# Recurrent gates on two row tiles of 64 partitions, with both gates' weights of a head side by side

## The reference

```python
def rg_lru(x, wa, ba, wx, bx, lam):            # x: (1, 1024, 1024); wa, wx: (16, 64, 64)
    xh = x.reshape(bsz, s, LRU_HEADS, LRU_HEAD_DIM)      # 16 heads of 64 channels
    r = jax.nn.sigmoid(jnp.einsum('bshi,hij->bshj', xh, wa).reshape(bsz, s, c) + ba)
    i = jax.nn.sigmoid(jnp.einsum('bshi,hij->bshj', xh, wx).reshape(bsz, s, c) + bx)
    log_a = -RG_C * r.astype(jnp.float32) * jax.nn.softplus(-lam.astype(jnp.float32))
    a = jnp.exp(log_a)
    mult = jnp.sqrt(-jnp.expm1(2.0 * log_a))
    b = mult * (i * x).astype(jnp.float32)
    ...                                        # h[t] = a[t] * h[t-1] + b[t], over the 1024 tokens
```

## Time and profile before

| | |
|---|---|
| median of 3 runs | 1730.13 us (1728.16 to 1732.98) |
| span of the profiled execution | 1726.5 us |
| TensorE busy | 1681.0 us, 97% |
| VectorE busy | 1225.3 us, 71% |
| ScalarE busy | 792.4 us, 46% |
| GpSimd busy | 516.6 us, 30% |
| mean HBM traffic over the span | 102 GB/s |

### The profile page before, as it was taken

One profiled execution on the slowest core, in us unless ns is written; L12 is line 12 of the kernel. 1 busy time (PEld: TensorE's weight loads), 2 busy tenths in 40 slices (PEclk: granted clock), 3 DMA queues, 4 the chain that ended last, 5 costly groups with the idle time before them and its releaser, 6 DMA issues.

```text
span 1726.5 us, 20915 instructions
## 1 busy us (share of the span) xinstructions
PE 1681.0 (97%) x7556; PEld 1383.3 (80%) x7556; DVE 1225.3 (71%) x1442; ACT 792.4 (46%) x1038; POOL 516.6 (30%) x284
## 2 busy tenths in 40 slices
PE   7999999999999999999999999998999999999998
PEld 6888878888877888888888888886878877777776
DVE  6577772259999888888888789885636365666554
ACT  5466541235764434343434455553322146676531
POOL 4221222200015555554552000003432242345320
PEclk8999999999999999999999999999999999999999
DMA  8111112152422232222223876651321320110251
GB/s 259 49 36 49 40 45 74 37 201 80 152 81 76 83 97 73 84 84 87 73 86 125 317 237 199 219 159 43 122 74 61 85 86 25 37 49 25 102 215 73
DMA packets 161095, 176.96 MB, mean 102 GB/s; under 512 B 13566, under 2 KB 114692, under 8 KB 161028
## 3 DMA queue, kind: packets, MB, share of 16 engines
q1 hardware_dynamic: 158724, 167.67, 30.3%
q10 hardware_dynamic: 2304, 8.39, 1.3%
HBM read 140.38 MB, written 35.65 MB: 102 GB/s over the span
## 4 chain that ended last, share of the span: by engine, by line
PE 82%; DVE 10%; ACT 4%; issue 1%; POOL 1%; DMA 1%; POOLq 0%; DVEq 0%; ACTq 0%; SPq 0%
PE ps L921 28%; PE ps L2398 24%; PE ps L2352 18%; PE ps L2618 4%; PE ps L2603 3%; PE ps L2648 2%; PE ps L2588 1%; DVE lat L2109 1%; PE ps L2576 1%; DVE pt_lo L2203 1%; DVE prob L2185 1%; POOL z_lo L1015 1%; PE ps L2279 1%; DVE square_dve L1636 0%; ACT pt_hi L1548 0%
## 5 line engine op out<-in xcount | busy, mean ns | idle before, releaser
L945 POOL TENSOR_TENSOR w_lo<-w_raw,w_hi 128x1024 fp32r<-128x1024 f32 x52 | 135.8, 2614 | 623.0 <-ACT w_hi L1044 623.0
L2398 PE MATMUL ps<-hop_hi_P,wop_hi_P 128*128 128x512 f32 x672 | 262.5, 391 | 4.7 <-DVE u L1853 3.3
L2398 PE MATMUL ps<-hop_hi_P,wop_lo_P 128*128 128x512 f32 x672 | 261.5, 389 | 0.0
L2398 PE MATMUL ps<-hop_lo_P,wop_hi_P 128*128 128x512 f32 x672 | 261.5, 389 | 0.0
L921 PE MATMUL ps<-h_hi,w_hi 128*128 128x512 f32 x752 | 235.1, 394 | 11.3 <-DVE h_lo L1621 7.8
L951 POOL TENSOR_TENSOR wop_lo_P<-pair_sum,wop_hi_P 128x512 fp32r<-128x512 f32 x90 | 135.9, 1510 | 354.5 <-ACT wop_hi_P L1055 354.5
L921 PE MATMUL ps<-h_lo,w_hi 128*128 128x512 f32 x752 | 232.9, 391 | 0.0
L921 PE MATMUL ps<-h_hi,w_lo 128*128 128x512 f32 x752 | 232.7, 391 | 0.0
L921 PEld LDWEIGHTS ps<-h_hi,w_hi 128*128 128x128 f32 x752 | 141.4, 189 | 43.3 <-issue 14.0
L921 PEld LDWEIGHTS ps<-h_lo,w_hi 128*128 128x128 f32 x752 | 142.1, 189 | 29.8
L921 PEld LDWEIGHTS ps<-h_hi,w_lo 128*128 128x128 f32 x752 | 142.0, 189 | 29.7
(11 more groups left out here) (350 smaller groups left out, 3337.9 us busy)
## 6 DMA issues: line engine op xcount, KB each, us to landing
pair_raw<-in_w_up SPq DMA_DIRECT2D x48, 512.0 KB, 4.6
w_raw<-in_w_in SPq DMA_DIRECT2D x46, 512.0 KB, 3.9
dn_raw<-gu_park SPq DMA_DIRECT2D x84, 256.0 KB, 3.9
dn_raw<-in_w_down SPq DMA_DIRECT2D x60, 256.0 KB, 3.1
gu_park<-up_cv SPq DMA_DIRECT2D x24, 512.0 KB, 2.6
out_raw<-in_w_out SPq DMA_DIRECT2D x30, 256.0 KB, 3.0
x_tok<-in_x SPq DMA_DIRECT2D x4, 1024.0 KB, 8.2
x_park<-xs SPq DMA_DIRECT2D x1, 4096.0 KB, 14.3
```

The costliest lines, as they stand in the source:

```text
L945: nc.gpsimd.tensor_tensor(lo[:, :], raw[:, :], hi[:, :].bitcast(f32), ALU.subtract).then_inc(w_lo_done, 1)
L2398: mm = nc.tensor.matmul(dst, w[q][:, k, :], x[q][:, k, :], start=a, stop=b, skip_group_check=True)
```

## The change

The gates of a tile are no longer a matmul with a block-diagonal matrix. Each of the two heads of a tile is a matmul of its own on 64 rows, with 128 columns of weights: 64 of `wa` and 64 of `wx`, side by side. The even head lies on partitions 0 to 63 and writes `ps[2]`, the odd one on partitions 64 to 127 and writes `ps[3]`; their matmuls are issued alternately. The number of matmuls stays 12 in a tile.

The columns of the odd head are in the other order (`which ^ e`), so that gate r of both heads comes out on the head's own partitions. Gate i then comes out on the other half, and ScalarE moves it: the two Tanh of 128 partitions become four of 64, and `bx` is kept with its halves exchanged. The block of zeros goes, and with it the memset, the wait for it and half of the columns of the gate weights that are cast and subtracted.

```diff
-        bd_raw = at("bd_raw", G0 + 8 * TILE, [2, LRU_TILES, P])
-        bd_hi = at("bd_hi", G0 + 10 * TILE, [2, P], f32r)
-        bd_lo = at("bd_lo", G0 + 11 * TILE, [2, P], f32r)
+        head_raw = at("head_raw", G0 + 8 * TILE, [LRU_TILES, P])
+        head_hi = at("head_hi", G0 + 10 * TILE, [P], f32r)
+        head_lo = at("head_lo", G0 + 11 * TILE, [P], f32r)
...
-            sp.wait_ge(const_done, BD_ZEROED)
             for which, wg in enumerate((lru_wa, lru_wx)):
                 heads = wg.rearrange("o (c e) i j -> (o e) i c j", e=2)
                 for e in range(2):
-                    sp.dma_start(bd_raw[64 * e:64 * e + 64, which, :, 64 * e:64 * e + 64],
-                                 heads[e]).then_inc(bd_in, 16)
+                    first = 64 * (which ^ e)
+                    sp.dma_start(head_raw[64 * e:64 * e + 64, :, first:first + 64], heads[e]).then_inc(bd_in, 16)
...
-            nc.gpsimd.memset(bd_raw[:, :, :, :], 0.0).then_inc(const_done, 1)
...
             def gate_weights(c, one):
-                nc.scalar.copy(bd_hi[:, :, :], bd_raw[:, :, one, :].rearrange("p w o n -> p w (o n)")
-                               ).then_inc(bd_hi_done, 1)
+                nc.scalar.copy(head_hi[:, :].unsqueeze(1), head_raw[:, one, :]).then_inc(bd_hi_done, 1)
 
             def gate_curves(c, one):
 
-                act.wait_ge(ri_done, 2 * c + 1)
-                nc.scalar.activation(scr[1][:, :], ps[2][:, :], ACT.Tanh, scale=0.5,
-                                     bias=half_ba[:, one]).then_inc(rt_done, 1)
+                even, odd = slice(0, 64), slice(64, P)
                 act.wait_ge(ri_done, 2 * c + 2)
-                nc.scalar.activation(scr[2][:, :], ps[3][:, :], ACT.Tanh, scale=0.5,
-                                     bias=half_bx[:, one]).then_inc(it_done, 1)
-
-                act.wait_ge(rt_done, c + 1)
+                for head, bank in ((even, ps[2]), (odd, ps[3])):
+                    nc.scalar.activation(scr[1][head, :], bank[head, :], ACT.Tanh, scale=0.5,
+                                         bias=half_ba[head, one]).then_inc(rt_done, 1)
+                for head, other, bank in ((even, odd, ps[2]), (odd, even, ps[3])):
+                    nc.scalar.activation(scr[2][head, :], bank[other, :], ACT.Tanh, scale=0.5,
+                                         bias=crossed_bx[other, one]).then_inc(it_done, 1)
+
+                act.wait_ge(rt_done, 2 * c + 2)
...
-            step(V.tensor_scalar(half_bx[:, :], vec[:, V_BX:V_BX + 8], 0.5, None, ALU.mult))
+            for head, other in ((slice(0, 64), slice(64, P)), (slice(64, P), slice(0, 64))):
+                step(V.tensor_scalar(crossed_bx[other, :], vec[head, V_BX:V_BX + 8], 0.5, None, ALU.mult))
...
             def second_parts(c, one):
                 dve.wait_ge(bd_hi_done, c + 1)
-                step(V.tensor_tensor(bd_lo[:, :, :], bd_raw[:, :, one, :].rearrange("p w o n -> p w (o n)"),
-                                     bd_hi[:, :, :].bitcast(f32), ALU.subtract))
+                step(V.tensor_tensor(head_lo[:, :].unsqueeze(1), head_raw[:, one, :], head_hi[:, :].bitcast(f32).unsqueeze(1),
+                                     ALU.subtract))
...
             def gates():
-                matmul3(pe, ps[2], bd_hi[:, 0, :], bd_lo[:, 0, :], xc_hi, xc_lo, True, True).then_inc(ri_done, 1)
-                matmul3(pe, ps[3], bd_hi[:, 1, :], bd_lo[:, 1, :], xc_hi, xc_lo, True, True).then_inc(ri_done, 1)
+                for w, x, first, last in ((head_hi, xc_hi, True, False), (head_hi, xc_lo, False, False),
+                                          (head_lo, xc_hi, False, True)):
+                    for t in (T1, T2):
+                        for head, bank in ((slice(0, 64), ps[2]), (slice(64, P), ps[3])):
+                            mm = nc.tensor.matmul(bank[:, t], w[head, :], x[head, t], start=first, stop=last)
+                            if last and t is T2:
+                                mm.then_inc(ri_done, 1)
```

More of the change, by code:

```diff
@@ L316, in program @@
         half_ba = const("half_ba", 8)
-        half_bx = const("half_bx", 8)
+        crossed_bx = const("crossed_bx", 8)
         half_ps = const("half_ps", 4)
@@ L360, in program @@
         const_done, vec_t, vec_done, setup_done = sem("const_done"), sem("vec_t"), sem("vec_done"), sem("setup_done")
-        IDENT, BD_ZEROED, SMALL_CONST, ALL_CONST = 1, 2, 7, 23
+        IDENT, SMALL_CONST, ALL_CONST = 1, 6, 22
         SIGN, POS_F, LAM_ABS, PARAMS = 4, 5, 6, 7
@@ L1685, in recur @@
                 step(V.tensor_scalar(scr[3][:, :], scr[1][:, :], -2.0, -1.0, ALU.mult, ALU.add))
-                dve.wait_ge(it_done, c + 1)
+                dve.wait_ge(it_done, 2 * c + 2)
                 step(V.scalar_tensor_tensor(out=scr[2][:, :], in0=scr[2][:, :], scalar=1.0, in1=xc,
@@ L2337, in _ @@
                 if n < 4:
-                    pe.wait_ge((conv_done, gelu_done, rt_done, it_done)[n], LRU_TILES)
+                    pe.wait_ge((conv_done, gelu_done, rt_done, it_done)[n], (1, 1, 2, 2)[n] * LRU_TILES)
                 else:
```

## The result

The changed kernel took 1746.18 us (median of 4 runs, 1744.07 to 1746.96), beside 1730.56 us for the kernel before (4 runs). The ratio is 1.0084, 95% interval 1.0067 to 1.0102: slower by 0.84%; the two medians lie 15.6 us apart. The forecast was 1737.4 us, slower by 0.42%, with a range from 1733 to 1748. The sign, the place and the mechanism were right; the forecast loss of 7.3 us is less than half of those 15.6.

A forecast was written before the change was run, and what follows sets the result against it. TensorE paces the kernel except at 248.76 us, where block 2 awaits a chain over ScalarE and VectorE. Loop +2.0, last two tiles +3.9 and slow clock +1.4 give +7.3 us: 1737.4 us, range 1733 to 1748.

The forecast's parts named there:

- Matmuls: Gates on TensorE: each pair of 64-row matmuls runs side by side in 0.227 us, 1.36 us per tile for 2.72.
- The serial rival: The two row tiles run one after the other, 26.18 us per loop iteration: +16.2 us, 1746.3 us; chance 0.18.
- The likeliest case: Whole kernel slower by 0.42%: 1737.4 us, with its own range 1735 to 1741 us; chance 0.50.
- Curves: Gate activations on ScalarE: two of 128 partitions become four of 64 at full time each, 2.00 us more per tile.
- The ring: Loop over recurrent tiles: ScalarE's curves, VectorE's recurrence to `xc_lo`, then gate matmuls set the pace, 24.82 us per iteration.
- The tail: From tile 6's first curve to block 2 of the short convolution: 37.5 us becomes 41.4, two tiles' extra curve time less 0.1.
- The gap and its clock: Ahead of block 2 TensorE idles 5.5 us instead of 1.5; the low clock behind it adds 1.4 us.
- Behind 248.8 us nothing takes it back: After block 2 starts TensorE has no gap, so the later start carries through to the total in full.

The follow-up runs named there:

- the first four experiments: Changed kernel with whole curves, 1724.14 us; kernel before with split curves, 1747.87; changed kernel with gate i whole, 1734.51; changed kernel with 18 unread matmuls, 1739.72.
- full_curves: The changed kernel with two Tanh of 128 partitions in place of its four of 64: 1724.14 us, ratio 0.9975 to the kernel before.

## Why the prediction was half right

*Matmuls: right.* 0.227 us per pair was taken, on no row of before; 1.59 us for the twelve was measured, where 1.36 to start and 1.52 to finish were expected. The serial rival gave 1746.3 us, the measured total to 0.1 us, and this is chance: its mechanism is excluded by the rows at 61.65 us. It was also this rival that set the upper end of the range, 1748 us. The likeliest case had 1735 to 1741 us as its own range, so that the measured time lies within the stated range is luck.

*Curves: right in kind, too small in size. This is the step that failed.* "ScalarE does 2.00 us more per tile" came from the start-to-start time of whole activations. Whole ones overlap: each lasts 1.12 us and the next starts after 1.00. Halves don't; each follows the end of the last, 1.135 us. The extra is 4.54 - 2.00 = 2.54 us. The row was there, in ScalarE's timeline of the kernel before:

```profile
1432.22 2.12 ACT L1501 CAST qr<-scr 64x1024 fp32r<-64x1024 f32 x2 [0.72 <-DVE scr L2129]
...
1447.34 1.93 ACT L1509 CAST qh_hi<-ps 128x1024 fp32r<-128x1024 f32 x2
```

A pair of 64-partition casts, as in the earlier trace rows, takes 2.12 us, a pair of 128 partitions in the same stretch 1.93. I had read a duration and priced it with a spacing.

*The ring: right.* The gate ring paces the loop, as forecast, and TensorE waits for `xc_lo`. With 0.54 more for the curves my 24.82 us become 25.36, and 25.22 was measured. The curve of tile 6 came at 215.74, not 213.3.

*The tail: right.* 41.4 us from there to block 2 were forecast, 42.55 measured, and 2 x 0.54 us of curves is the difference. Block 2 was 9.5 us later, not 5.9. Of the 3.6 us between, that one price alone would make 8 x 0.54 = 4.3; the first curve came 0.58 us earlier (64.04 us), which takes most of the surplus back.

*The gap and its clock: right at its place, missed elsewhere.* The gap was forecast at 5.5 us and was 4.24, since `xc_lo` of tile 7 came 0.5 us later and the matmuls behind its 2.2 us gap ran slowly. It cost 2.1 us for the 1.4 assumed. But the forecast looked for a low clock only there. The clock also fell behind the 2.21 us gap ahead of the gates of tile 7, near 500 us, and behind the 2.13 us gap at 87.43 us. There it made TensorE the last to arrive (0.50 us of wait on ScalarE at 112.91) and cost 0.4 us: from first curve to first curve that iteration takes 25.65 us, for 25.22. The length of a pause alone doesn't decide. Busy time from 90 to 94 us, of the kernel after, of the one with the 18 matmuls, and of the one with the heads one after the other (columns as in rows 2; the clock is 0.71, 1.00 and 0.57):

```profile
90.00:94.00 4.00, 4.00 (x14) 3.12 (x13) 2.28 (x2) 3.90 (x5) 1.35 (x1) 0.71 0.30 89
```

```profile
90.00:94.00 4.00, 4.00 (x19) 3.32 (x18) 2.69 (x3) 3.92 (x4) 1.98 (x1) 1.00 0.12 33
```

```profile
90.00:94.00 4.00, 4.00 (x12) 2.80 (x11) 2.97 (x3) 3.09 (x3) 2.24 (x1) 0.57 0.06 16
```

The pauses ahead of these stretches were 2.13, 2.11 and 1.57 us. The second, shorter than the first by 0.02 us, left the clock at 1.00, and the third, the shortest, was followed by the lowest clock; another of 1.57 us in the same kernel, at 192.85 us, was not. The Trainium skill (TensorE: Matmul & The Clock Gate, "Why this matters for your kernels") warns of pauses between bursts of matmuls as what brings the clock down. The trace agrees where the low clock stands behind a pause, but pauses shorter than those that the page warns of were enough here in some profiles and not in others.

*"Behind 248.8 us nothing takes it back": right for the delay itself*, by the kernel with 49 matmuls more: 9.4 us of delay cost 9.6 us in the pair of runs with the higher clock, and more in the other. The 1.9 us that come back near 1630 us in the profiles are a dip of the kernel before.

## What to carry to other kernels

Price the change on the ring that it lies on, not on the busiest engine: TensorE was 97% busy, and 0.9 us per tile saved on it bought nothing, while 2.5 us on an engine that was 46% busy set the time. When one instruction becomes two on half the partitions, take the price from such a pair in the timeline, start to start, and not from a mean duration. And count a gap on TensorE with the slow matmuls that may stand behind it. When two profiles are compared place by place, go on to the end: a sum that fits by the middle can be chance.

## What the runs showed of the hardware

- Activations on 64 partitions take as long as on 128 (1.11 us each) and, in the pairs seen here, don't overlap with each other: 1.135 us start to start for 1024 columns, against 1.00 us. Why they don't stays open.
- Two row tiles of 64 rows run side by side: 12 matmuls of 512 columns in 1.59 us, against 2.72 us for 12 of 128 rows.
- TensorE starts a matmul of the free row tile ahead of earlier ones in the queue that wait for theirs (the seventh ahead of the fourth, 88.89 and 89.11 us). The Trainium skill (TensorE: Matmul & The Clock Gate, "The mechanism") says that matmuls keep their order in start and end; for the starts this trace does not agree.
- One kernel's executions differ by dips of the clock that come in some and not in others. Of the 17 of the kernel before beside the first four experiments, 11 took 1727.3 to 1729.6 us with a mean clock of 0.992 or 0.993, five 1732.9 to 1734.5 us with 0.988, and one lay between. The full_curves kernel did the same (1722.3 to 1724.1 at 0.993, three at 1727.3 to 1732.4 at 0.986 to 0.989). The dip near 500 us is worth 3.0 us. It is missing only in the profiles of the kernel before and of full_curves, and stands in all the others, that of an execution of 1728.99 us too. TensorE pauses 0.76 us there in the changed kernel and 0.80 us in the kernel before, so no longer pause explains it. What decides whether it comes stays open, and with it how much of it belongs to the change.
